# On-chip row forming by exact bf16 splits, from the eighth group of experts on, in a fused trunk-layer kernel

## The reference

```python
def moe(h, w_router, b_router, w_gate_e, w_up_e, w_down_e, w_gate_s, w_up_s, w_down_s):
    bsz, l, d = h.shape
    t = h.reshape(bsz * l, d)
    scores = jax.nn.sigmoid((t @ w_router).astype(jnp.float32))
    _, idx = lax.top_k(scores + b_router.astype(jnp.float32), TOP_K)
    sel = jnp.take_along_axis(scores, idx, axis=-1)
    wts = sel / jnp.sum(sel, axis=-1, keepdims=True) * ROUTED_SCALE
    combine = jnp.sum(jax.nn.one_hot(idx, N_EXPERTS, dtype=jnp.float32) * wts[..., None], axis=1)
    hg = jnp.einsum('td,edf->tef', t, w_gate_e)
    hu = jnp.einsum('td,edf->tef', t, w_up_e)
    act = jax.nn.silu(hg) * hu * combine[..., None].astype(t.dtype)
    routed = jnp.einsum('tef,efd->td', act, w_down_e)
    shared = (jax.nn.silu(t @ w_gate_s) * (t @ w_up_s)) @ w_down_s
    return (routed + shared).reshape(bsz, l, d)
```

## Time and profile before

| | before |
|---|---|
| median of 3 runs | 956.34 us |
| the profiled execution's own time | 954.98 us |
| its span | 953.3 us |
| TensorE busy | 911.8 us (96%) |
| VectorE, ScalarE, GpSimd busy | 424.9, 188.0, 94.9 us |
| moved | 322 MB, mean 338 GB/s |
| of it by gathers and scatters | 22.22 MB |

### The profile page before, as it was taken

One profiled execution on the slowest core, in us unless ns is written; L12 is line 12 of the kernel. 1 busy time (PEld: TensorE's weight loads), 2 busy tenths in 40 slices (PEclk: granted clock), 3 DMA queues, 4 the chain that ended last, 5 costly groups with the idle time before them and its releaser, 6 DMA issues.

```text
span 953.3 us, 13253 instructions
## 1 busy us (share of the span) xinstructions
PE 911.8 (96%) x5001; PEld 488.0 (51%) x5001; DVE 424.9 (45%) x769; ACT 188.0 (20%) x309; POOL 94.9 (10%) x198
## 2 busy tenths in 40 slices
PE   5899999999999999999999999989999989899996
PEld 2455567676555687544444444434445454354532
DVE  4129966534762336463333333223233323323267
ACT  3150601212100013112212212111121211212121
POOL 2000000000000000202122111111111201111100
PEclk9999999999999999999999999999999999999999
DMA  9998463625686356799999999999999999999996
GB/s 343 356 403 332 133 206 140 227 89 177 237 293 268 124 249 235 280 400 370 422 418 421 421 419 420 419 421 420 420 421 419 420 423 418 423 420 421 417 416 252
DMA packets 85034, 322.04 MB, mean 338 GB/s; under 512 B 10084, under 2 KB 38936, under 8 KB 56040
## 3 DMA queue, kind: packets, MB, share of 16 engines
q1 hardware_dynamic: 70368, 289.43, 76.4%
q0 software_dynamic: 9216, 22.22, 6.0%
q10 hardware_dynamic: 5384, 9.51, 2.7%
HBM read 298.36 MB, written 34.11 MB: 349 GB/s over the span
## 4 chain that ended last, share of the span: by engine, by line
PE 86%; DMA 7%; DVE 2%; issue 2%; ACT 1%; SPq 1%; DVEq 0%; POOLq 0%
PE bank L624 25%; PE bank L1910 21%; PE bank L653 13%; PE bank L2096 4%; PE bank L2082 4%; PE bank L610 3%; DMA arena<-expert_rows 3%; DMA arena<-in_w_mod_dram 3%; PE bank L2002 2%; PE bank L2124 2%; PE bank L604 2%; PE bank L577 2%; PE bank L642 1%; ACT arena L635 1%; DVE arena L638 1%
## 5 line engine op out<-in xcount | busy, mean ns | idle before, releaser
L624 PE MATMUL bank<-arena 128*32 128x512 f32 (+2 forms) x1568 | 258.4, 600 | 8.0 <-issue 8.0
L1910 PE MATMUL bank<-arena 128*128 128x384 f32 x640 | 209.9, 487 | 2.4 <-ACT arena L1697 2.4
L624 PEld LDWEIGHTS bank<-arena 128*32 128x32 f32 (+2 forms) x1568 | 90.2, 124 | 171.3 <-issue 171.1
L1910 PEld LDWEIGHTS bank<-arena 128*128 128x128 f32 x640 | 120.3, 190 | 85.6 <-issue 5.2
L653 PE MATMUL bank<-arena 128*32 128x512 f32 (+2 forms) x784 | 131.5, 596 | 4.9 <-issue 4.2
L653 PEld LDWEIGHTS bank<-arena 128*32 128x32 f32 (+2 forms) x784 | 43.1, 122 | 69.8 <-issue 69.1
L658 DVE SCALAR_TENSOR_TENSOR arena<-bank,arena 128x512 f32<-128x512 f32 x36 | 27.0, 751 | 106.5 <-PE bank L653 106.3
L666 ACT ACTIVATE arena<-arena 128x1024 f32<-128x1024 f32 x36 | 41.3, 1148 | 163.1 <-DVE arena L662 159.3
L463 DVE SCALAR_TENSOR_TENSOR arena<-arena 128x2048 f32<-128x2048 f32 x28 | 64.6, 2348 | 18.5 <-DMA arena<-in_w_mod_dram 17.4
L638 DVE TENSOR_TENSOR arena<-arena,bank 128x256 f32<-128x256 f32 x36 | 21.9, 607 | 85.7 <-ACT arena L635 85.7
L570 DVE TENSOR_TENSOR arena<-arena 128x288 f32<-128x288 f32 (+3 forms) x64 | 22.0, 380 | 82.2 <-POOL arena L741 41.2
(11 more groups left out here) (262 smaller groups left out, 796.1 us busy)
## 6 DMA issues: line engine op xcount, KB each, us to landing
arena<-in_w_up_e_dram SPq DMA_DIRECT2D x64, 1024.0 KB, 29.3
arena<-in_w_down_e_dram SPq DMA_DIRECT2D x64, 1024.0 KB, 29.2
arena<-in_w_gate_e_dram SPq DMA_DIRECT2D x64, 1024.0 KB, 27.3
arena<-in_w_mod_dram SPq DMA_DIRECT2D x24, 1024.0 KB, 7.4
arena<-in_w_in_dram SPq DMA_DIRECT2D x22, 1024.0 KB, 7.7
expert_rows<-arena SPq DMA_DIRECT2D x6, 2048.0 KB, 22.1
arena<-expert_rows SPq DMA_DIRECT2D x12, 1024.0 KB, 21.8
arena<-in_w_out_dram SPq DMA_DIRECT2D x4, 1024.0 KB, 5.3
```

Of the source, the lines that this page charges most:

```text
L624: ins = pe.matmul(bank[off:off + width, :], x_T[:, k, off:off + width], w[:, :, k, :], start=(k == 0), stop=(k == KT - 1))
L1910: ins = pe.matmul(ps[:, 0:TOK], w[:, k, P * (n % 2):P * (n % 2) + P], hT[:, k, :], start=(k == 0), stop=(k == KT - 1))
```

## The change

Four things are done.

1. h2 is split into three bf16 arrays, `high`, `middle` and `lowest`, whose sum is h2 exactly. ScalarE makes `high` in the loop's iteration 0 and `middle` in iteration 2, VectorE subtracts in iterations 1 and 3 (each of these four instructions is 128 x 3072; `lowest` takes the place of h2). The two new arrays and 12 KB per partition of SBUF for them come from a smaller scratch space of the dynamic DMAs (4096 bytes where 16384 is the default).
2. `ON_CHIP` becomes every group from 7 to 35: 29 groups instead of 6. 23 gathers go, 7 stay.
3. `rows_from_tokens` multiplies each of the three parts by a bf16 one-hot: 8 x 3 x 3 = 72 bf16 matmuls instead of 24 float32 ones (48 instructions).
4. The tables are bf16 too. Token numbers, output rows and weights are split into parts that bf16 holds exactly, eight columns instead of four; one more matmul (`ones_half` by `far`) adds the constant. VectorE sums the parts (`row_numbers`, two reductions more), GpSimd copies twice per expert (`pick`), and `values(t)` has five more dependent instructions.

Some semaphores are merged (`step_done`, `consts`), which keeps their waits.

```diff
-FAR = 8192.0
+FAR = 4096.0
...
-ON_CHIP = [15, 19, 23, 27, 31, 34]
+ON_CHIP = list(range(7, NQ))
...
+        high, middle = [at(take(NT * D // 2), NT * D // 2).bitcast(BF16).rearrange("p (t d) -> p t d", t=NT)
+                        for n in range(2)]
+        lowest = h2.rearrange("p t d -> p (t d)").bitcast(BF16).rearrange("p (t d) -> p t d", t=NT)[:, :, 0:D]
...
         def pick(pool, b, s, e):
-            return pool.tensor_copy(qv[:, b % 2, s], vals[:, :, bass.ds(e, 1), :].rearrange("p t e v -> p t (e v)"))
+            pool.tensor_copy(qv[:, b % 2, s, :, 3:7], traits[:, :, bass.ds(e, 1), :].rearrange("p t e v -> p t (e v)"))
+            return pool.tensor_copy(qplace[:, b % 2, s, :], place_of[:, :, bass.ds(e, 1)].rearrange("p t e -> p (t e)"))
...
         def table(pe, b, s, off, width):
             for o, w in [(32, 32), (64, 64)] if (off, width) == (32, 96) else [(off, width)]:
+                pe.matmul(banks[7][o:o + w, 0:8], ones_half[:, o:o + w], far, start=True, stop=False)
                 for t in range(NT):
-                    ins = pe.matmul(banks[7][o:o + w, 0:4], onehot[b][:, t, o:o + w], qv[:, b % 2, s, t, :],
-                                    start=(t == 0), stop=(t == NT - 1))
+                    ins = pe.matmul(banks[7][o:o + w, 0:8], onehot[b][:, t, o:o + w], qv[:, b % 2, s, t, :],
+                                    start=False, stop=(t == NT - 1))
             return ins
...
+        def row_numbers(dve, x, b, times):
+            dve.tensor_reduce(row_sums, banks[7][:, 0:4].rearrange("p (j v) -> p v j", v=2), AX.X, ALU.add)                .then_inc(x["summed"], 1)
+            dve.tensor_scalar(of_seq[:, 0, b:b + 1], banks[7][:, 0:1], float(CTX), None, ALU.is_lt)
+            dve.tensor_scalar(of_seq[:, 1, b:b + 1], banks[7][:, 0:1], float(CTX), None, ALU.is_ge)
+            dve.tensor_reduce(wt[:, b:b + 1], banks[7][:, 4:7], AX.X, ALU.add)
+            dve.wait_ge(x["summed"], times)
+            return dve.tensor_copy(rows_i[:, b, :], row_sums)
...
         def rows_from_tokens(pe, b, part):
             for k in part:
                 for t in range(NT):
-                    ins = pe.matmul(banks[k // 4][:, P * (k % 4):P * (k % 4) + P], h2[:, t, P * k:P * k + P],
-                                    onehot[b][:, t, :], start=(t == 0), stop=(t == NT - 1))
+                    for n, rows in enumerate((high, middle, lowest)):
+                        ins = pe.matmul(banks[k // 4][:, P * (k % 4):P * (k % 4) + P], rows[:, t, P * k:P * k + P],
+                                        onehot[b][:, t, :], start=(t == 0 and n == 0), stop=(t == NT - 1 and n == 2))
             return ins
...
+                if i in (0, 2):
+                    act.wait_ge(S["split_done"], i)
+                    act.activation((high, middle)[i // 2], h2, ACT.Copy).then_inc(S["split_done"], 1)
...
+                if i in (1, 3):
+                    dve.wait_ge(S["split_done"], i)
+                    dve.tensor_tensor((h2, lowest)[i // 2], h2, (high, middle)[i // 2], ALU.subtract)\
+                        .then_inc(S["split_done"], 1)
...
-                link(dve.tensor_scalar(vals[:, t, :, 3], scores[:, t, :], weight_sum[:, one], ROUTED_SCALE,
+                dve.tensor_scalar(traits[:, t, :, 0], rank[:, t, :], low, None, ALU.add)
+                link(dve.tensor_scalar(scores[:, t, :], scores[:, t, :], weight_sum[:, one], ROUTED_SCALE,
                                        ALU.mult, ALU.mult))
+                for part in (1, 2):
+                    link(dve.tensor_copy(traits[:, t, :, part], scores[:, t, :]))
+                    link(dve.tensor_tensor(scores[:, t, :], scores[:, t, :], traits[:, t, :, part], ALU.subtract))
+                link(dve.tensor_copy(traits[:, t, :, 3], scores[:, t, :]))
...
-    nc = _bacc.Bacc("TRN2", target_bir_lowering=False, num_devices=1)
+    nc = _bacc.Bacc("TRN2", target_bir_lowering=False, num_devices=1, dynamic_dma_scratch_size=4096)
```

More of the change, by code:

```diff
@@ L316, in program, with row_table @@
         mod_rows = at(a_rows, 3, 512)
-        vals = at(a_rows, NT, NE, 4)
-        onehot = [at(a, NT, ROWS) for a in (a_rows + 768, a_rows + 768 + NT * ROWS)]
-        places = [at(a, TOK) for a in (a_rows + 768, a_rows + 768 + NT * ROWS)]
+        place_of = at(a_rows, NT, NE)
+        traits = at(a_rows + NT * NE, 2 * NT * NE).bitcast(BF16).rearrange("p (t e v) -> p t e v", t=NT, v=4)
+        a_hot = a_rows + 3 * NT * NE
+        def row_table(a):
+            return at(a, NT * ROWS // 2).bitcast(BF16).rearrange("p (t r) -> p t r", t=NT)
+        onehot = [row_table(a) for a in (a_hot + NT * ROWS, a_hot + 3 * NT * ROWS // 2)]
+        places = [at(a, TOK) for a in (a_hot, a_hot + NT * ROWS)]
+        qplace = at(a_hot + 2 * NT * ROWS, 2, 2, NT)
+        assert a_hot + 2 * NT * ROWS + 4 * NT <= a_rows + 1536
         a_z = take(512)
@@ L357, in program @@
         part_f = at(take(1), 1)
-        far = at(take(2), 2)
+        far = at(take(4), 4).bitcast(BF16)
+        row_sums = at(take(2), 2)
+        low = at(take(1), 1)
+        low_i = at(take(1), 1).bitcast(I32)
         most_f = at(take(1), 1)
         most_i = at(take(1), 1).bitcast(I32)
-        tok_far = at(take(2 * NT), 2, NT)
+        static = at(take(2 * NT), 2, NT)
         of_seq = at(take(8), 2, 4)
@@ L453, in unit_arrived, with step @@
             eng.wait_ge(unit_in[n % UNITS], 16 * (n // UNITS + 1))
+        def step(eng, name):
+            eng.wait_ge(S["step_done"], STEPS.index(name) + 1)
         def add_modulation(eng, g, k, link):
@@ L904, in numbers @@
                     n = i - ADDED
-                    dve.tensor_scalar(token_of[:, n:n + 1], banks[7][:, 1:2], FAR, None, ALU.add)
-                row_numbers(dve, i % 4).then_inc(x["rows_ready"], 1)
+                    dve.tensor_reduce(token_of[:, n:n + 1], banks[7][:, 0:4].rearrange("p (j v) -> p v j", v=2)[:, 0, :],
+                                      AX.X, ALU.add)
+                row_numbers(dve, x, i % 4, i + 1).then_inc(x["rows_ready"], 1)
             def x_half(i):
@@ L1061, in dve_spill @@
                 dve.wait_ge(x["picked"], n + 1)
[L1062 removed]
+                mark(dve, onehot[2], 2, 0, 0, ROWS).then_inc(x["onehot_done"], 1)
                 dve.wait_ge(x["tab_done"], n + 1)
[L1064 removed]
+                row_numbers(dve, x, NQ % 4, n + 1).then_inc(x["rows_ready"], 1)
                 dve.wait_ge(x["xtr_done"], n + 1)
@@ L1401, in vector_part_a @@
                 link(dve.tensor_scalar(key_col[0:n, :], key_col[0:n, :], -PRIOR, None, ALU.add))
+            for b in range(2):
+                for s in range(2):
+                    dve.tensor_copy(qv[:, b, s, :, 0:2], static.rearrange("p v t -> p t v"))
+                    dve.tensor_copy(qv[:, b, s, :, 2:3], part_f.unsqueeze(1).to_broadcast([P, NT, 1]))
+                    link(dve.memset(qv[:, b, s, :, 7:8], 0.0))
             dve.wait_ge(S["router_in"], 32)
@@ L1435, in vector_part_b @@
             full(dve, job)
-            free(dve.scalar_tensor_tensor(out=vals[:, :, :, 0],
+            free(dve.scalar_tensor_tensor(out=place_of,
                                           in0=bank(job)[:, 0:NT * NE].rearrange("p (t e) -> p t e", t=NT), scalar=1.0,
@@ L1742, in _ @@
                     act.activation(f[:, d], f[:, d], ACT.Exp, scale=1.0 / GATE_NORM).then_inc(S["exp_ready"], 1)
-            act.wait_ge(S["conv_done"], 1)
+            step(act, "conv_done")
             for name, dst, scale in (("k", kT, 1.0), ("q", qT, float(P) ** -0.5)):
@@ L1772, in _ @@
                 free(ins, job)
-            act.wait_ge(S["ro_ready"], 1)
+            step(act, "ro_ready")
             act.activation(head_rms, head_rms, ACT.Sqrt).then_inc(S["sqrt_ready"], 1)
@@ L1780, in _ @@
                     act.dma_start(norm2_rows[r:r + 1, :], norm2_w[:, 512 * q:512 * q + 512]).then_inc(S["norm2_in"], 16)
-            act.wait_ge(S["state_done"], 1)
+            step(act, "state_done")
             act.dma_start(new_state[0, 0].rearrange("w h k v -> k (w h) v"), new_st).then_inc(S["out_done"], 16)
@@ L2065, in _ @@
             project("gbc", NH + 2, NH)
-            pe.wait_ge(S["rows_normed"], 1)
+            step(pe, "rows_normed")
             for h in range(NH):
@@ L2072, in _ @@
             project("gbg", KT, 6)
-            pe.wait_ge(S["gla_ready"], 1)
+            step(pe, "gla_ready")
             for n in range(KT):
```

73 lines of the change are left out of this document (37 added, 36 removed).

## The result

The changed kernel takes 980.38 us (median of 4 runs, 980.15 to 980.73), the kernel before 956.01 us beside it (4 runs): ratio 1.0257 [1.0245, 1.0269], slower by 24.4 us. The forecast was 985 us, 973 to 1010.

A forecast was written before the change was run, and what follows sets the result against it. TensorE, almost without a break in the loop, was taken as the bound. Loop +25.0, before it +2.6, tail +1.3 sum to +28.9 us: 985 us against 956.34, range 973 to 1010 (8 in 10).

The forecast's parts named there:

- The step: Rows on chip: one 128-column bf16 matmul to the next takes 0.056 us, so 72 take 4.0 us against 5.4 in float32.
- Rivals 1: Row matmuls step longer than 0.056 us; at 0.081, 1037 us; chance 0.10 for 0.075 or more, 0.08 for 0.062 to that.
- 3 (0.03): Row matmuls step at 0.03 us like 64-column ones, the DMA queue ends the loop, about 941 us; chance 0.02.
- The period and the loop: Groups 0 to 33: on-chip period 15.2 us instead of 17.23, 28 of them; loop 513.8 us against 488.8, +25.0.
- Rival 2: Other engines end the period's middle: row_numbers' wait, second pick or a split, 0.5 us per group, 1002 us; chance 0.05.
- One reading behind this: Gathered groups: the 2.45 us between gate_up and down are activation latency; TensorE waits for DVE's product in 25 groups, 0.3-0.6 us.
- The worth of the gathers: In the loop, 23 fewer gathers can give back at most 11.6 us: 8.0 of waits and 3.6 of slow clock.
- the 4.26 of the prediction: Kernel before: a group with float32 rows formed on chip costs TensorE 4.26 us more than a gathered one.
- Ahead of the loop: Before the loop: longer values(t), picks and row_numbers delay group 0's gather, behind which all of TensorE stands; +2.6 us.
- Tail: After the loop: group 35's rows on chip cost 1.9 us, of which 0.6 is hidden; +1.3 us.
- Splits, small instructions, scratch: In the loop: all covered, nothing; uncovered 13 us for splits, 0 to 0.5 per group, at most 2 for five groups.
- Rival 4: No change: TensorE's extra work falls into weight waits that the trace hides as busy; 956 us, chance 0.02.

The follow-up runs named there:

- bf16, fourteen spread: Changed kernel with 14 groups on chip (9, 10, 12, 14, 15, 17, 19, 20, 23, 25, 27, 28, 30, 35) instead of 29: 949.71 us, ratio 0.9939.
- high part only: Changed kernel with rows formed from the high part alone, 24 bf16 matmuls per group instead of 72: 937.61 us, ratio 0.9815.
- The last experiment: Changed kernel with the tokens' weights in one bf16 part instead of three, four dependent VectorE steps fewer per values(t): 979.08 us, ratio 1.0246.

## Why the prediction was right

**The step, on which all hung: right.** 36 matmuls in 2.01 us are 0.0558 us each, predicted 0.056. By shape, the changed kernel's row formation and its tables from 380 us on (busy us, mean ns):

```profile
L634 PE MATMUL bank<-arena 128*128 128x128 bf16 x2088 | 126.2, 219 | 0.0
```

```profile
L634 PEld LDWEIGHTS bank<-arena 128*128 128x128 bf16 x2088 | 119.1, 98 | 1.6 <-issue 0.8
...
L598 PEld LDWEIGHTS bank<-arena 128*32 128x32 bf16 x75 | 3.7, 94 | 2.0 <-issue 2.0
L598 PEld LDWEIGHTS bank<-arena 128*64 128x64 bf16 x90 | 3.6, 111 | 1.9 <-issue 1.9
L598 PEld LDWEIGHTS bank<-arena 128*96 128x96 bf16 x27 | 1.9, 124 | 1.2 <-issue 1.2
```

Each load is shown with 98 ns and each matmul with 219 from start to modelled end, and still a pair passes every 56: both overlap, and what counts is the step. It went with the streamed columns here, 0.03 us for 64 and 0.056 for 128. Rivals 1 (a longer step) and 3 (0.03) are out. The Trainium skill ("TensorE: Matmul & The Clock Gate", section "Back-to-back issue gap") gives 81 ns for 128-column matmuls in a stream of load and matmul pairs, and 56 ns only for the isolated gap; these 2088 pairs keep the shorter one in runs of 36, so the page's rule for streams doesn't hold for this stream.

**The period and the loop: right.** 15.12 us for 15.2 on chip, 88.24 us (495.27 - 407.03) for 88.2 of the gathered groups. The loop grew by 22.7 us instead of 25.0; 28 x 0.08 = 2.2 of the difference is the round 15.2. Rival 2 is out: TensorE was busy for all of the 400 us shown above, with no wait for DVE behind a table. One reading behind this was wrong, without harm to the sum. The row is of the weight-load engine; TensorE itself waited for DVE's product in 10 groups, not 25 (430 to 890 us, kernel before):

```profile
PE bank L642 <- DVE arena L638: 2.6, 10, 0.3
```

The 2.45 us of a gathered group are thus TensorE's own table and transposes where the table is long (0.88 us), and the latency where it is short; both are about equally long. That a shorter table gives nothing there held: with the bf16 tables and six groups on chip, TensorE waits for the product in 27 groups, 13.7 us in the same stretch.

**The worth of the gathers: right.** All of the 11.6 us of waits and slow clock came back, and no more, as the sum had it. What the runs add is where it stops, in one table: for each kernel the groups n that count in the loop, TensorE's sum (451.4 plus 2.15 n in bf16, 3.97 n in float32; before's six at the 4.26 of the prediction), the queue's line (489.9 - 0.87 n), and the loop measured.

| kernel | n | TensorE | queue | loop |
|---|---|---|---|---|
| before, none on chip | 0 | 451.4 | 489.9 | 489.9 |
| bf16, six | 6 | 464.3 | 484.7 | 485.0 |
| before (float32, six) | 6 | 477.0 | 484.7 | 488.8 |
| bf16, fourteen spread | 13 | 479.3 | 478.6 | 480.4 |
| bf16, thirteen | 13 | 479.3 | 478.6 | 481.4 |
| float32, thirteen | 13 | 503.0 | 478.6 | 504.1 |
| bf16, twenty | 20 | 494.4 | 472.5 | 494.6 |
| changed kernel | 28 | 511.6 | 465.5 | 511.5 |
| high part only (a period of 13.0 without waits) | 28 | about 452 | 465.5 | 464.5 |
| float32, twenty-eight | 28 | 562.6 | 465.5 | 562.6 |

The loop is the larger of the two sums, to about 1 us where they lie 13 us or more apart, and up to 4 above it where they are closer. Why it is above was not tried; that weights are only two to three groups ahead may be the reason. The 2.15, the 0.87 and the 3.97 are fitted to the rows with n of 0, 6 and 28; the rows of thirteen and twenty test them, and fourteen and twenty were forecast by them. The changed kernel moved 28 groups where 12.7 balance: the last 15 cost 2.15 us each and gave nothing back.

**Ahead of the loop: the size roughly, and that by luck; the path wrong.** +1.8 us (405.25 to 407.03) for +2.6. The step that failed is "where TensorE already waits 0.63 us", with "Behind this gather stands all of TensorE". The row of 402.99 in the earlier trace rows is of the weight-load engine. TensorE's own rows of the kernel before have the filler until 403.18 and the transposes from 403.02, with no idle time between:

```profile
395.19 7.99 PE L2124 MATMUL bank<-arena 128*128 128x512 f32 x18
403.02 1.06 PE L604 MATMUL bank<-arena 128*128 128x128 f32 x8
```

And the gather, issued at 397.29 instead of 394.50, 2.8 us later, still lands in time, also because it takes less: 6.8 us from issue to landing, 8.4 before. What makes the 1.8 us is something else: two waits for DVE ahead of the gather, 0.57 and 1.42, which the kernel before doesn't have, less 0.7 for the shorter tables. The remaining 0.5 is there before the first instruction of `values` that was changed, as the same step of `choose(0)` shows, first before, then now:

```profile
366.23 0.23 DVE L1380 MAX8 arena<-arena 128x8 f32<-128x64 f32 x1
```

```profile
366.75 0.23 DVE L1419 MAX8 arena<-arena 128x8 f32<-128x64 f32 x1
```

The executions of all kernels here differ by about as much at this place (the first write of h2's copy is at 348.1 to 349.3 us), with the old code and with the new, so it is not counted to the change. The last experiment took away 1.5 of the two waits' 2.0 us.

**Tail: right in kind.** 60.05 us from down 33's end to the end of the span, 59.2 before: +0.8 for +1.3. Group 35's rows on chip are in it now; the two waits for the reading back, 0.6 together, went, and the end is TensorE's.

**Splits, small instructions, scratch: nearly nothing, as said.** One may be seen: ACT's first split (426.92, 2.75 us) stands ahead of ACT's work for iteration 1, and DVE's product comes late there. It is one of these five waits of TensorE, 430 to 920 us, with 0.57; the other four are in groups 2 to 5, gathered ones with the shorter table:

```profile
PE bank L666 <- DVE arena L662: 2.3, 5, 0.7
```

Groups 0 and 1 take 36.38 us, 36.33 before, so nothing of it is left in the time. Those of groups 2 to 5 take 12.94 to 12.98 us each, as before, so the other three splits aren't seen either. The scratch alone is 0.9998. Rival 4 (no change) is out with the ratio of 1.0257.

**The sum.** 22.7 + 1.8 + 0.8 = +25.3 us of span (953.3 to 978.6), where 28.9 were forecast; the median grew by 24.4. All three terms were too large, so none hid another's error. The range was stated wider than its terms: 15.0 a period, +1.5 and no tail give 985 - 5.6 - 1.1 - 1.3 = 977 and not 973, and a step of 0.060 with one slow stretch gives 995 and not 1000. The result lies within the narrower one too.

## What to carry to other kernels

When work can be moved from a busy queue to a busy engine, price one unit on both sides (here 2.15 us of TensorE against 0.87 of queue) and stop where the two sums meet; past that point each unit costs its full price, however cheap it was made. When the last wait for weights vanished from the chain here, the gain was at its end, and no more followed. And read the idle time of the engine you mean: a weight load that starts late behind a long matmul is no wait of TensorE.

## What the runs showed of the hardware that was not expected

- bf16 weight loads of 128 columns are shown with 98 ns, shorter than those of 96 (124) and 64 (111); in float32 the loads grow with the columns, 110, 137 and 190 ns for 32, 64 and 128 (L648 of the changed kernel), while the transposes' loads of 128 are shown with 140 (L627). The Trainium skill ("TensorE: Matmul & The Clock Gate", section "Weight-path perf modes — Fast Weight Load (FWL) and DoubleRow") has a faster load for exactly 128 weights of a type that isn't float32. The 98 against 124 agrees with it.
- In the kernel before, the granted clock was 0.63 in the 3.4 us behind a wait of 2.84 us and 0.59 behind one of 2.60, but 1.00 behind one of 2.53. With the old list in bf16 it was 0.54 behind a wait of 2.45 us and 1.00 behind one of 2.17. So the length of the one wait didn't decide it. In the changed kernel, with TensorE gapless, it was 1.00 in every stretch of the loop that was read.
- The two gathers ahead of the loop, the same data each time, took 7.5 to 8.4 us from issue to landing in the kernel before, 5.7 to 6.8 in the changed one and 6.8 to 8.1 with the weights in one part. What sets this was not tried.
